# The token-shift mix for the gate projection: from VectorE to ScalarE and GpSimd

## The reference, cut to what matters

```python
xx = token_shift(h) - h
xm = h[None] + xx[None] * mu.astype(F32)[:, None, None, :]
rkvz = jnp.einsum("pbtd,pde->pbte", xm[:4], w_rkvz)
r, k, v, z = rkvz[0], rkvz[1], rkvz[2], rkvz[3]
logw = -jax.nn.softplus(-(w0 + jnp.tanh(xm[4] @ w1) @ w2)) - 0.5
a = jax.nn.sigmoid(a0 + (xm[5] @ a1) @ a2)
```

## Time and profile before

| | |
|---|---|
| median of 3 runs | 4256.69 us (4254.74 to 4256.97) |
| the profiled execution | 4253.47 us |
| its span, first to last instruction | 4251.6 us |
| TensorE busy | 90% of the span |
| VectorE busy | 46% |
| ScalarE busy | 34% |
| GpSimd busy | 3% |
| mean granted clock of TensorE | 0.972 |

### The profile page before, as it was taken

How to read it: one execution, slowest core, us unless ns; L and a number is a source line. 1 busy time by engine, 2 the same in 40 slices (tenths; PEclk the granted TensorE clock), 3 DMA queues, 4 the chain that set the end, 5 groups by cost and what they waited for, 6 DMA issues and landing times.

```text
span 4251.6 us, 53880 instructions
## 1 busy us (share of the span) xinstructions
PE 3837.3 (90%) x21962; PEld 2283.9 (54%) x21962; DVE 1948.1 (46%) x4078; ACT 1429.4 (34%) x2596; POOL 139.9 (3%) x151
## 2 busy tenths in 40 slices
PE   2998899999899799999989879999999987999998
PEld 2554456556455356556546536556555644556554
DVE  7345554454245554454325464454442546454452
ACT  1333343343233233243224333343333333333242
POOL 0000000000000100000000010000000001000000
PEclk8998999999999899999999989999999998999999
DMA  7222110101212210110132120010012213010101
GB/s 308 60 88 63 32 32 26 31 31 41 84 47 91 65 37 26 32 31 22 42 98 61 60 81 26 27 33 25 31 56 74 61 60 86 27 31 26 32 31 40
DMA packets 269421, 229.01 MB, mean 54 GB/s; under 512 B 15548, under 2 KB 251256, under 8 KB 266104
## 3 DMA queue, kind: packets, MB, share of 16 engines
q1 hardware_dynamic: 266872, 217.18, 16.5%
q0 software_dynamic: 2304, 8.39, 0.5%
HBM read 208.76 MB, written 16.78 MB: 53 GB/s over the span
## 4 chain that ended last, share of the span: by engine, by line
PE 73%; DVE 15%; ACT 8%; issue 2%; DMA 1%; SPq 0%; DVEq 0%; ACTq 0%
PE bank L514 13%; PE bank L380 12%; PE bank L594 7%; PE bank L587 7%; PE bank L473 7%; PE bank L456 4%; PE bank L583 3%; PE bank L413 3%; PE bank L377 3%; DVE xm L1218 3%; PE bank L619 2%; PE bank L636 2%; PE bank L630 2%; PE bank L504 1%; DMA xm<-in_ada_w 1%
## 5 line engine op out<-in xcount | busy, mean ns | idle before, releaser
L514 PE MATMUL bank<-xm,wring 128*128 128x512 f32 x2048 | 1084.7, 631 | 68.8 <-ACT arena L876 35.4
L380 PE MATMUL bank<-arena,wring 128*128 128x512 f32 x1280 | 580.2, 593 | 14.0 <-ACT xm L722 10.2
L514 PEld LDWEIGHTS bank<-xm,wring 128*128 128x128 f32 x2048 | 336.0, 191 | 321.9 <-issue 174.8
L380 PEld LDWEIGHTS bank<-arena,wring 128*128 128x128 f32 x1280 | 230.8, 190 | 259.0 <-issue 254.4
L910 ACT COPY arena<-bank 128x512 f32<-128x512 f32 x320 | 187.5, 586 | 451.2 <-PE bank L583 451.2
L587 PE MATMUL bank<-arena 128*128 128x128 f32 x2560 | 338.1, 275 | 0.0
L594 PE MATMUL bank<-arena 128*128 128x128 f32 x2560 | 312.0, 275 | 0.0
L587 PEld LDWEIGHTS bank<-arena 128*128 128x128 f32 x2560 | 311.0, 192 | 0.0
L473 PE MATMUL bank<-wring,yT 128*128 128x512 f32 x608 | 277.6, 620 | 32.4 <-DVE yT L1251 22.3
L594 PEld LDWEIGHTS bank<-arena 128*128 128x128 f32 x2560 | 298.7, 192 | 0.0
L1326 DVE TENSOR_TENSOR arena<-bank,wmask 128x256 f32<-128x256 f32 x320 | 135.9, 425 | 302.4 <-PE bank L587 302.4
(11 more groups left out here) (256 smaller groups left out, 5026.1 us busy)
## 6 DMA issues: line engine op xcount, KB each, us to landing
wring<-in_rw_w_rkvz SPq DMA_DIRECT2D x128, 512.0 KB, 3.7
wring<-in_ev_w_in SPq DMA_DIRECT2D x96, 512.0 KB, 5.5
xm<-in_ada_w SPq DMA_DIRECT2D x16, 1536.0 KB, 12.3
wring<-in_ev_w_out SPq DMA_DIRECT2D x32, 512.0 KB, 8.0
wring<-in_rw_w_out SPq DMA_DIRECT2D x32, 512.0 KB, 3.5
xm<-in_x POOLq DMA_DIRECT2D x16, 512.0 KB, 5.7
arena<-in_x SPq DMA_DIRECT2D x16, 512.0 KB, 5.2
residual_scratch<-arena SPq DMA_DIRECT2D x4, 2048.0 KB, 7.5
```

Source lines behind the costliest of these rows:

```text
L380: mm = pe.matmul(pj[:, :], w[:, k, :], hT[:, k, 1:1 + TB], start=(k == 0), stop=(k == KC - 1))
L514: mm = pe.matmul(pj[:, :], w[:, k, :], xmv[MIX_OF[i - 2]][:, k, :], start=(k == 0), stop=(k == KC - 1))
```

## The change

Mix Z is no longer made by VectorE. After `lora_act` ScalarE makes `xx * mu` for the 8 tiles of slot 1, and GpSimd adds `hT` to each, as both do for mix A. TensorE's first Z projection of a block waits tile by tile for `xz_r`; `xm_r` counts three mixes a block instead of four. VectorE waits for all 8 adds before it clears `r_N`, since `r_N` and later tiles lie where `hT` was.

```diff
-        xm_k xm_r xa_m xa_r lo_in ...
+        xm_k xm_r xa_m xa_r xz_m xz_r lo_in ...
@@ lora_down (PE)
-                pe.wait_ge(S["xm_r"], b * 4 + 1)
+                pe.wait_ge(S["xm_r"], b * 3 + 1)
@@ rwkv_proj (PE)
-                        if i > 2 and k == 0:
-                            pe.wait_ge(S["xm_r"], b * 4 + i - 1)
+                        if i in (3, 4) and k == 0:
+                            pe.wait_ge(S["xm_r"], b * 3 + i - 1)
+                        if i == 5 and first:
+                            pe.wait_ge(S["xz_r"], b * KC + k + 1)
@@ rwkv_prepare (PE), and so for each later rwkv_proj in it
-                rwkv_proj(b, pp, q, RN - KC, RN - KC + 2)
+                rwkv_proj(b, pp, q, RN - KC, RN - KC + 2, not prev)
@@ layer 1, after lora_act(b) (ACT)
+                for k in range(KC):
+                    act.mul(xmv[1][:, k, :], yTv[:, k, :], PB[:, ROWS_B["mu"] + MU_Z * KC + k:ROWS_B["mu"] + MU_Z * KC + k + 1])\
+                        .then_inc(S["xz_m"], 1)
@@ mixes (DVE)
                 mix(0, MU_V)
-                mix(1, MU_Z)
                 V.wait_ge(S["r_save"], (b + 1) * 16)
@@ rwkv_prepare (DVE)
                 if not prev:
+                    V.wait_ge(S["xz_r"], (b + 1) * KC)
                     V.memset(r_N, 0.0).then_inc(S["r_n0"], 1)
@@ end of the block's work (POOL)
+                for k in range(KC):
+                    gp.wait_ge(S["xz_m"], b * KC + k + 1)
+                    gp.tensor_tensor(xmv[1][:, k, :], xmv[1][:, k, :], hT[:, k, 1:1 + TB], ALU.add).then_inc(S["xz_r"], 1)
```

More of the change, by code:

```diff
@@ L215, in build @@
         h_kd h_kt h_kdT h_qd h_win h_pp h_po h_pooled h_s h_sz h_o h_osq h_ss h_rn h_y op_ready op_std ob
-        xm_k xm_r xa_m xa_r lo_in lo_pe lo_r rp_ready rp_ev w2_free r_ksq ms_ready ms_free r_sig rk_sum v_tok v_tr y_mean y_cent y_var r_rs r_scan r_dec r_arbk r_rk sc_ready
+        xm_k xm_r xa_m xa_r xz_m xz_r lo_in lo_pe lo_r rp_ready rp_ev w2_free r_ksq ms_ready ms_free r_sig rk_sum v_tok v_tr y_mean y_cent y_var r_rs r_scan r_dec r_arbk r_rk sc_ready
         sc_free r_n0 r_n tr_l l_r inv1 invw invt invtt inv2 invT ch_x ch_xs ch_u ch_us ch_z ch_m ch_pm y_ready y_sb
@@ L551, in rwkv_prepare @@
                 mm.then_inc(S["v_tr"], 1)
-                rwkv_proj(b, pp, q, RN - KC + 2, RN - KC + 5)
+                rwkv_proj(b, pp, q, RN - KC + 2, RN - KC + 5, not prev)
                 pe.wait_ge(S["r_arbk"], u + 1)
@@ L555, in rwkv_prepare @@
                     if h:
-                        rwkv_proj(b, pp, q, RN - KC + 5, RN - KC + 6)
+                        rwkv_proj(b, pp, q, RN - KC + 5, RN - KC + 6, not prev)
                     pe.wait_ge(S["ms_free"], 1 + u * 3 + 1 + h)
@@ L571, in rwkv_prepare @@
                 for h in range(2):
-                    rwkv_proj(b, pp, q, RN - KC + 6 + h, RN - KC + 7 + h)
+                    rwkv_proj(b, pp, q, RN - KC + 6 + h, RN - KC + 7 + h, not prev)
                     pe.wait_ge(S["r_n"], u * 2 + h + 1)
```

## The result

The changed kernel takes 4267.38 us (median of 9, 4265.67 to 4268.71) against 4256.97 (median of 9, 4254.74 to 4260.10): the ratio is 1.0024, interval 1.0014 to 1.0034. It is slower by 10.4 us. The profiled executions are 4266.43 and 4253.47, 13.0 apart. Measured again, with other executions of the kernel before beside it, it was 4267.69 against 4258.9, ratio 1.0025 (1.0014 to 1.0035).

What follows compares the result with a forecast made beforehand. TensorE, busy 90%, was taken as the engine to keep fed, waiting on VectorE's chain in layer 1's head. A 1.9 us delay there becomes 3.4 a block: 4256.7 + 13.6 = 4270.3 us, range 4255 to 4274.

Steps and rivals of the forecast that it cites:

- Where the time could come from: Head of layer 1: of Z's 5.4 us a block, only 0.9 is on the path, since the scan needs the second sigmoid.
- The multiplies: ScalarE behind L822: eight multiplies 0.63 us apart take 5.04 against 4.58 idle, so R is emptied 0.4 later.
- The adds and the turns: GpSimd's eight adds alternate with VectorE, last until about 463, and make scan, L1265 and L1266 wait 0.6, 0.9 and 0.9.
- the uncertain one: L1266 on VectorE, one SBUF input: counted as blocked by the eighth add for 0.9 us; without it the delay is 1.0.
- The head: Head of layer 1: L1268 ends 2.4 - 0.5 = 1.9 us later, and TensorE leaves the head as late, each block.
- What becomes of it: Between blocks: clock changes stay fixed, so a small delay is pulled back and a larger one moves the block to the next distance.
- One step of 3.4 a block: Each of four blocks takes 3.4 us longer, 13.6 in all; chance 0.46.
- The boundary: Delay of the head above which a block moves to the next distance instead of being pulled back; estimated at 1.1 us.
- How the step is filled: TensorE before L559: the wait grows enough that a short half-clock stretch can follow, costing up to 1.7; 1.9 + 1.7 nears 3.4.
- The time: Whole kernel: 4256.7 + 13.6 = 4270.3 us, with 4267 to 4273 as the likeliest case's own range.
- the 13.6 us: Total slowdown over the run: four blocks, each 3.4 us longer, added to the median of the kernel before.

Runs made afterwards that it cites:

- e6_zsplit: Kernel before, but VectorE makes six tiles of Z ahead of the scan and the last two behind L1271; 4254.43 us, ratio 0.9993.
- e1_noread: Changed kernel with GpSimd's eight adds for Z replaced by eight writes of a constant to the same tiles; 4260.49 us, ratio 1.0000 to the kernel before.
- e5_muls: Kernel before with ScalarE's eight multiplies added, results unused, VectorE still making Z; 4261.11 us, ratio 1.0000.
- e2_late08: Kernel before with one VectorE write of 900 elements ahead of the scan, to delay the head; 4258.64 us, ratio 0.9994.
- c_before: Kernel before, unchanged, measured and profiled once more; 4256.78 us, ratio 0.9999.
- e4_late20: Kernel before with one VectorE write of 2300 elements ahead of the scan, to delay the head; 4267.98 us, ratio 1.0030.

## Why the prediction was right, point by point

- *Where the time could come from.* The chain showed 5.4 us of Z, the timelines 0.9. The scan started 0.43 earlier with the change and 0.90 earlier in e6_zsplit, where ScalarE is not burdened. Right.
- *The multiplies.* Predicted 0.63 apart and R 0.4 late; measured 0.61 and 0.48. The 0.1 that I took off for the copy's own end is not there: the first multiply starts 0.03 behind it.
- *The adds and the turns.* Predicted until 461 alone, about 463 with the turns, and waits of 0.6, 0.9 and 0.9; measured 463.09, and 0.55, 0.89 and 0.94. The sixth add was under way when the scan came, as reckoned. Alone an add takes 1.08, not 1.0, the first 1.63, not 2.0, and the fourth 1.26; that these errors cancel, and the sixth add stands where I had put it, is luck. L1266, the uncertain one, did wait: 1.48 instead of 0.54. Here the trace agrees with the Trainium skill's "SBUF — State Buffer", "Who interferes with whom", which names tensor_scalar among the operations that can take both ports.
- *The head.* 1.9 predicted, 1.96 measured, in all four blocks. e1_noread and e5_muls show that nothing else has a part in it.
- *What becomes of it.* One step of 3.4 a block was predicted, and 3.30, 3.40 and 3.43 measured. I had drawn this from shifts of 0.04 us in the earlier trace rows, which are read to 0.01; it held at 25 times the size, since e2_late08's 1.00 lengthens a distance by 0.06 at most where it does not bring a step. The boundary was put at 1.1: at 1.00 two of three blocks stayed, at 1.73 none. It is no clean line, though: blocks also slipped at delays of 0 and -0.42, each of them behind a stray stretch of half clock, which cost 1.5 in c_before, more than the boundary.
- *How the step is filled.* This sub-step was wrong. I had a short stretch of half clock follow the wait before L559. There is none: that wait grows only from 1.02 to 1.12, and TensorE's granted clock is 1.00 from 470 to 480 in the changed kernel as before. The half clock is longer 600 us later, where block 0 ends and the next begins. Something like it comes at a delay of 2.45 (e4_late20), where it follows a wait of 2.08 before L542 and costs 1.7.
- *The time.* 4270 predicted, 4267.4 measured. Two things make the 13.6 us too large. The last block has no whole step, since the program ends before it is filled: 10.1 by the distances and 2.7 behind the last tanh, 13.0 in the profiled pair. And it was added to a median that probably held slipped blocks already, as c_before's profile has one; the 10.4 between the medians fits that, without showing it. The profiled execution's distance of 3.2 us from the median, about one step, was the hint, and I took it for plain scatter.

That the moments of the clock's changes do not move with the kernel, which the prediction concluded from two rows, is borne out by the 13 profiles: the changes stand whole steps apart, and with mix A on the same engine every tanh comes in the same place between them, to 0.2 us. With the rule of "TensorE: Matmul & The Clock Gate", Part 1, of the Trainium skill, that the monitor runs freely, these traces agree. What stays open is why the clock falls for a stray stretch in one execution and not in the next.

## What to carry to other kernels

Ask of a helper not how long its work takes but whose instructions stand still meanwhile: a mix moved from VectorE to GpSimd saved 0.68 us a tile, and each add took 0.9 from what VectorE did then, where VectorE was busy with operands in SBUF. Of an instruction on the chain, only the part up to the next thing that the follower waits for can be gained: 0.9 of 5.4 us here. And where TensorE's clock falls in every round of a loop, measure the distance of the rounds: small gains and losses can vanish or become a step, so a change is worth judging by its place in one round as well as by the total.

## What the runs showed that I had not expected

- The kernel before itself takes 1037.6 or 1041.0 us for one and the same block, in one execution (c_before), at a mean granted clock of 0.98 or 0.97, and the slower block has one stray stretch of half clock while TensorE is busy.
- GpSimd's add of 512 elements from two SBUF tiles takes 1.08 us alone; a scan that meets it takes 1.77 instead of 1.22, and the add that waited for the scan 2.18.
- Giving VectorE eight more mixes and freeing GpSimd made the head's first part 2.1 us shorter.
